# Order of the sliding attention's products, and 32-wide array strips for the RWKV head sums

## The reference, cut to what matters

```python
def swa_mixer(h, w_qkv, q_gain, k_gain, sinks, w_o, cos, sin):
    qkv = h @ w_qkv                      # 16 query heads, 4 key heads, 4 value heads of 64
    q = rope_slice(rms_norm(q, q_gain), cos, sin, 0)   # rope on the first 16 of 64 features
    k = rope_slice(rms_norm(k, k_gain), cos, sin, 0)
    # scores q k / 8, kept where |i - j| <= 128, softmax with a sink per head, times v
    return o @ w_o

# rwkv7_mixer
    kk = heads(k * k_k)
    kk = kk / jnp.maximum(jnp.sqrt(jnp.sum(kk * kk, axis=-1, keepdims=True)), 1e-12)
    # per direction:
    bonus = jnp.sum(rf * kd * rkf, axis=-1, keepdims=True) * vf    # 16 heads of 64
```

## Time and profile before

| | us |
|---|---|
| median of 3 runs | 1478.11 (1477.13 to 1478.13) |
| the profiled execution | 1479.16 |
| its span, first to last instruction | 1476.8 |
| PE busy in the span | 1418.9 |
| DVE, ACT, POOL busy | 549.3, 302.4, 115.1 |
| mean granted TensorE clock | 0.985 of 2.4 GHz |

### The profile page before, as it was taken

The page is one execution under the profiler, slowest core; times in us unless marked ns, Lnnn a source line. Parts: engine busy times, 40 slices in busy tenths (PEclk is TensorE's granted clock), DMA queues, the critical chain, the costliest instruction groups (busy, mean ns, idle before and its releaser), DMA issues.

```text
span 1476.8 us, 21440 instructions
## 1 busy us (share of the span) xinstructions
PE 1418.9 (96%) x9420; PEld 1027.3 (70%) x9420; DVE 549.3 (37%) x1032; ACT 302.4 (20%) x631; POOL 115.1 (8%) x180
## 2 busy tenths in 40 slices
PE   7999998999999997899999999999999989999999
PEld 6867567588884444468887458857788666888843
DVE  4677411121220045423333038448444372333300
ACT  3221102110110013411121003603433331212100
POOL 5654000000000000000000000022000000000000
PEclk9999999999999997999999999999999999999999
DMA  8343233244344334044434443400000222434432
GB/s 308 134 171 114 113 115 115 91 159 170 122 165 170 115 129 156 1 148 164 168 123 165 170 172 114 172 1 2 4 31 31 91 84 114 153 133 172 153 132 86
DMA packets 16605, 181.94 MB, mean 123 GB/s; under 512 B 1649, under 2 KB 3825, under 8 KB 5889
## 3 DMA queue, kind: packets, MB, share of 16 engines
q1 hardware_dynamic: 14320, 175.12, 31.4%
q10 hardware_dynamic: 2192, 5.46, 1.0%
HBM read 179.52 MB, written 1.05 MB: 122 GB/s over the span
## 4 chain that ended last, share of the span: by engine, by line
PE 89%; DVE 7%; ACT 3%; issue 1%; DMA 0%; POOL 0%; DVEq 0%; POOLq 0%
PE banks L1212 38%; PE banks L1475 15%; PE banks L1243 13%; PE banks L1222 4%; PE banks L1705 2%; PE banks L1426 2%; PE banks L1694 2%; PE banks L1198 1%; DVE weight_ring L2527 1%; PE banks L1563 1%; ACT weight_ring L1099 1%; ACT weight_ring L1104 1%; PE banks L1825 1%; PE banks L1776 1%; PE banks L1551 1%
## 5 line engine op out<-in xcount | busy, mean ns | idle before, releaser
L1212 PE MATMUL banks<-hT,weight_ring 128*128 128x256 f32 x2240 | 487.3, 379 | 1.0 <-DVE hT L1971 1.0
L1212 PEld LDWEIGHTS banks<-hT,weight_ring 128*128 128x128 f32 x2240 | 424.6, 190 | 62.2 <-issue 1.4
L1475 PE MATMUL banks<-weight_ring,arena 128*128 128x512 f32 x528 | 227.4, 592 | 0.0
L2256 DVE SCALAR_TENSOR_TENSOR arena<-banks,prm,arena 128x255 f32<-128x255 f32 x220 | 96.1, 478 | 305.4 <-ACT arena L944 197.2
L1475 PEld LDWEIGHTS banks<-weight_ring,arena 128*128 128x128 f32 x528 | 100.1, 190 | 124.1 <-issue 123.9
L1243 PE MATMUL banks<-weight_ring,arena 128*128 128x512 f32 x288 | 127.4, 600 | 3.0 <-ACT arena L1129 1.2
L1980 DVE TENSOR_TENSOR x<-x,banks 128x512 f32<-128x512 f32 x28 | 19.1, 686 | 276.5 <-PE banks L1475 192.2
L1243 PEld LDWEIGHTS banks<-weight_ring,arena 128*128 128x128 f32 x288 | 54.9, 192 | 69.7 <-issue 68.2
L944 ACT ACTIVATE arena<-banks,prm 128x256 f32<-128x256 f32 x66 | 33.6, 559 | 242.0 <-PE banks L1212 207.8
L1212 PE MATMUL banks<-arena,weight_ring 128*128 128x256 f32 x320 | 71.9, 386 | 0.0
L785 ACT ACTIVATE xn<-x 128x512 f32<-128x512 f32 x32 | 20.0, 627 | 242.5 <-DVE x L1980 236.6
(11 more groups left out here) (383 smaller groups left out, 1390.1 us busy)
## 6 DMA issues: line engine op xcount, KB each, us to landing
weight_ring<-in_wall SPq DMA_DIRECT2D x81, 2048.0 KB, 8.2
weight_ring<-in_wall SPq DMA_DIRECT2D x2, 1024.0 KB, 7.2
x<-in_x_tok ACTq DMA_DIRECT2D x2, 512.0 KB, 4.4
arena<-in_mem_tok SPq DMA_DIRECT2D x1, 1024.0 KB, 17.4
arena<-in_wall SPq DMA_DIRECT2D x1, 1024.0 KB, 5.0
arena<-in_wide SPq DMA_DIRECT2D x2, 512.0 KB, 4.9
out_y<-x ACTq DMA_DIRECT2D x4, 256.0 KB, 2.0
arena<-in_masks ACTq DMA_DIRECT2D x1, 896.0 KB, 9.9
```

The lines of the kernel that those rows point to most:

```text
L1212: ins = mm(b_(n)[:, j * T:(j + 1) * T], lhsT=wc[:, kb * 512 + c0:][:, :P], rhs=xT[:, kb, :], start=kb == 0, stop=kb == blocks - 1)
L1475: ins = mm(b_(tile_group(name, tt, c)), lhsT=actT[:, fb, tt * P:(tt + 1) * P], rhs=wc[:, (fb % 4) * D + c * 512:][:, :512], start=fb == 0, ...
L2256: ins = stt(out, src, col(f"fcw{i}", tap * nb_ + fb), out, ALU.mult, ALU.add)
```

## The change

Two parts.

Sliding attention. The qkv weights are laid out as keys and values (chunk 0), query heads 0 to 7 (chunk 1), query heads 8 to 15 (chunk 2). PE's order becomes: chunks 0 and 1 of tile 0, tile 1's norm transposes, chunks 0 and 1 of tile 1, chunk 2 of tile 0; then the transposes of the keys and of query blocks 0 and 1, for both tiles at once; then half of chunk 2 of tile 1 (`last_heads`), scores of units 0 and 1, the other half, and the loop. Query blocks 2 and 3 are transposed in the loop behind `window_columns(1)`. DVE's norm and rope become `head_norms(tt, h0, count)`: twelve heads (keys and eight queries) of each tile before the keys are copied out, eight heads of tile 0 before unit 0's maximum, eight heads of tile 1 between `window_p(0)` and `window_max(2)`. `w_sq` has a buffer for each tile, so that ACT no longer waits for `qk_sums`. ACT copies the last qkv group out between the exponentials of units 0 and 1. The groups have named banks.

RWKV. `headsel` gets 32 columns a block (the two heads of a block at 2 (fb mod 2), the rest zero), and `kk_ss` sums each of four pairs of blocks on its own strip of 32 array columns, into rows 32q of the bank. `kk_bc` takes its 32 rows from strip q and writes bank q. `bonus` works as `kk_ss` does, with 256 moving columns; DVE copies its 256 columns to `bonus_rows`, two transposes (`tx_bonus`, in level 2 of step 0) turn them to tokens, and DVE copies 32 columns of them to `r_bon` in level 3. POOL's clearing of the states waits for `tx_bonus` instead of `bonus`. The constants `cst` and `back` grow by 64 KB each.

```diff
@@ order of the groups
-    out += [("qkv_a", 2), ("tx_swa_b", 2), ("qkv_b", 4), ("k_tr", 1), ("q_tr", 4)]
-    out += [("sw_s0", 1, "pair0"), ("sw_s1", 1, "pair1")]
+    out += [("qkv_a", 2, 0, 1), ("tx_swa_b", 2, 2, 3), ("qkv_b", 3, 4, 5, 7), ("k_tr", 1, 6), ("q_tr_a", 2, 2, 3)]
+    out += [("sw_s0", 1, "pair0"), ("sw_s1", 1, "pair1"), ("qkv_c", 1, 6)]
     for u in range(8):
-        out += [(f"sw_s{u + 2}", 1, f"pair{u % 2}")] * (u < 6) + [(f"sw_t{u}", 1, "pair2")]
+        out += [(f"sw_s{u + 2}", 1, f"pair{u % 2}")] * (u < 6) + [(f"sw_t{u}", 1, "pair2")] + [("q_tr_b", 2, 7, 6)] * (u == 1)
@@ ScalarE
-            for u in range(2):
-                window_exp(u)
+            window_exp(0)
+            qkv_out(*QKV_ORDER[5])
+            window_exp(1)
@@ TensorE
+            def last_heads(blocks):
+
+                n, wc = tile_group("qkv", 1, 2), chunk("qkv", 2)
+                if blocks.start == 0:
+                    free(n)
+                for kb in blocks:
+                    ins = mm(b_(n), lhsT=h_mid[:, kb, P:T], rhs=wc[:, kb * 512:(kb + 1) * 512], start=kb == 0, stop=kb == KB - 1)
+                if blocks.stop == KB:
+                    ins.then_inc(psum_full, 1)
+
+            for q in range(2):
+                pe.wait_ge(*when_read(norm_group("swa", 0) + q))
+            for c in (0, 1):
+                heads_of_tile(0, c)
+            norm_transposes(5, 1, norm_group("swa", 1), xn)
+            for q in range(2):
+                pe.wait_ge(*when_read(norm_group("swa", 1) + q))
+            for c in (0, 1):
+                heads_of_tile(1, c)
+            heads_of_tile(0, 2)
+            pe.wait_ge(roped, 2)
+            turn_heads(G["k_tr"], 0)
+            for q in range(2):
+                turn_heads(turned_q(q), 256 + 256 * q)
...
+            last_heads(range(4))
+            pe.wait_ge(*when_read(G["k_tr"]))
             for u in range(2):
                 window_scores(u)
+            last_heads(range(4, KB))
             for u in range(8):
                 if u < 6:
                     window_scores(u + 2)
                 if u == 7:
                     swa_out(0, range(4))
                 window_columns(u)
+                if u == 1:
+                    pe.wait_ge(roped, 4)
+                    for q in (2, 3):
+                        turn_heads(turned_q(q), 256 + 256 * q)
...
-            for fb in range(KB):
-                ins = mm(b_(n)[0:16, 0:T], lhsT=c_("headsel", KB * 16)[:, 16 * fb:16 * fb + 16],
-                         rhs=kk_sq[:, fb * T:(fb + 1) * T], start=fb == 0, stop=fb == KB - 1)
+            for j in range(2):
+                for q in range(4):
+                    fb = 2 * q + j
+                    ins = mm(b_(n)[32 * q:32 * q + 32, 0:T], lhsT=c_("headsel", KB * 32)[:, 32 * fb:32 * fb + 32],
+                             rhs=kk_sq[:, fb * T:(fb + 1) * T], start=j == 0, stop=j == 1, tile_position=(0, 32 * q))
...
-                n = G["kk_bc"] + q
-                free(n)
-                for j in range(2):
-                    ins = mm(b_(n)[:, j * T:(j + 1) * T], lhsT=back[:, (2 * q + j) * P:][:, :P],
-                             rhs=rn_out, start=True, stop=True)
-                ins.then_inc(psum_full, 1)
+                free(G["kk_bc"] + q)
+            for j in range(2):
+                for q in range(4):
+                    rows_ = slice(32 * q, 32 * q + 32)
+                    ins = mm(b_(G["kk_bc"] + q)[:, j * T:(j + 1) * T], lhsT=back[rows_, j * P:(j + 1) * P],
+                             rhs=rn_out[rows_, :], start=True, stop=True, tile_position=(32 * q, 0))
+                    if j:
+                        ins.then_inc(psum_full, 1)
...
-            for tt in range(TT):
-                for fb in range(KB):
-                    ins = mm(b_(n)[:, tt * 16:(tt + 1) * 16], lhsT=rks[:, fb * T + tt * P:][:, :P],
-                             rhs=bonus_sel[:, 16 * fb:16 * fb + 16], start=fb == 0, stop=fb == KB - 1)
+            for j in range(2):
+                for q in range(4):
+                    fb = 2 * q + j
+                    ins = mm(b_(n)[32 * q:32 * q + 32, 0:T], lhsT=bonus_sel[:, 32 * fb:32 * fb + 32],
+                             rhs=rks[:, fb * T:(fb + 1) * T], start=j == 0, stop=j == 1, tile_position=(0, 32 * q))
...
+                    if (j, lv) == (0, 2):
+                        pe.wait_ge(*when_read(G["bonus"]))
+                        transposes(G["tx_bonus"], [bonus_rows[:, tt * P:(tt + 1) * P] for tt in range(TT)])
@@ VectorE
+            for tt in range(TT):
+                head_norms(tt, 0, 12)
             n = G["k_tr"]
             dve.wait_ge(psum_full, n + 1)
             ts_(w_kT, b3(n, 2, T), col("k_col"), None, ALU.mult).then_inc(bank_sem(n), 1)
...
+            head_norms(0, 12, 8)
...
             for u in range(8):
                 window_p(u)
+                if u == 0:
+                    head_norms(1, 12, 8)
                 if u < 6:
                     window_max(u + 2)
+                if u == 1:
+                    for q in (2, 3):
+                        n = turned_q(q)
+                        dve.wait_ge(psum_full, n + 1)
+                        ts_(w_qT[:, 2 * q:2 * q + 2, :], b3(n, 2, T), col("q_col"), None, ALU.mult).then_inc(bank_sem(n), 1)
...
-            V.tensor_copy(r_bon, b_(n, 32)).then_inc(bank_sem(n), 1)
+            V.tensor_copy(bonus_rows, b_(n, T)).then_inc(bank_sem(n), 1)
...
+                    if (j, lv) == (0, 3):
+                        n = G["tx_bonus"]
+                        dve.wait_ge(psum_full, n + 1)
+                        V.tensor_copy(r_bon.rearrange("p (t q c) -> p t q c", t=TT, q=4),
+                                      b3(n, TT, P).rearrange("p t (q c) -> p t q c", q=4)[:, :, :, 0:4]).then_inc(bank_sem(n), 1)
```

More of the change, by code:

```diff
@@ L2302, in _, with head_norms @@
             dve.wait_ge(in_swc, 16)
[L2303 to L2305 removed]
+            def head_norms(tt, h0, count):
+                for c in ((0, 1) if h0 == 0 else (2,)):
                     dve.wait_ge(*when_read(tile_group("qkv", tt, c)))
[L2307 to L2309 removed]
+                part, root = qss[:, 20 * tt + h0:][:, :count], qrs[:, 20 * tt + h0:][:, :count]
+                do(V.tensor_reduce(part, h64b(w_sq[:, tt, HD * h0:][:, :HD * count]), AX, ALU.add))
@@ L2310, in _ @@
                 do(ts_(part, part, 1 / HD, EPS, ALU.mult, ALU.add))
-                do(newton_root(qrs[:, 20 * tt:20 * tt + 20], part, qrt))
-                qk = h64b(qkv[:, tt, 0:1280])
-                do(tt_(qk, qk, spread(qrs[:, 20 * tt:20 * tt + 20], HD), ALU.mult))
-                rot = 2 * HALF_ROT
-                step(tt_(qk[:, 0:16, 0:rot], qk[:, 0:16, 0:rot], tiled(row("q_gain", rot), 16), ALU.mult))
-                do(tt_(qk[:, 16:20, 0:rot], qk[:, 16:20, 0:rot], tiled(row("k_gain", rot), 4), ALU.mult))
+                do(newton_root(root, part, qrt[:, 0:count]))
@@ L2317, in _ @@
+                qk = h64b(qkv[:, tt, HD * h0:][:, :HD * count])
+                do(tt_(qk, qk, spread(root, HD), ALU.mult))
+                rot, keys = 2 * HALF_ROT, 4 if h0 == 0 else 0
+                if keys:
+                    step(tt_(qk[:, 0:keys, 0:rot], qk[:, 0:keys, 0:rot], tiled(row("k_gain", rot), keys), ALU.mult))
+                do(tt_(qk[:, keys:count, 0:rot], qk[:, keys:count, 0:rot], tiled(row("q_gain", rot), count - keys), ALU.mult))
                 x1, x2 = qk[:, :, 0:HALF_ROT], qk[:, :, HALF_ROT:rot]
-                cos_ = tiled(swc[:, SWC["cos"] + tt * HALF_ROT:][:, :HALF_ROT], 20)
```

111 lines of the change are left out of this document (52 added, 59 removed).

## The result

The changed kernel takes 1459.3 us (median of 4 runs, 1458.0 to 1459.5) against 1478.1 for the kernel before: 18.8 us less, a ratio of 0.9872 with a 95% interval of 0.9855 to 0.9889. The forecast was 1465.4 with a range from 1460.5 to 1472.5, so the gain was larger than forecast, and outside the range. The profiled execution took 1459.16 us, with a span of 1457.3.

The account below looks back on a forecast made before the run. TensorE was taken as the bound (busy 96% of the span), with VectorE bounding the window loop. Attention -4.0 and RWKV strips -8.75 make -12.75 us, from 1479.16 for the profiled execution to a median of 1465.4; range 1460.5 to 1472.5.

Parts of the forecast that it names:

- Start: Sliding attention, before tile 1's norm transposes: two products instead of three no longer cover DVE's eviction, cost +1.0 us.
- first norms: Sliding attention: DVE's twelve-head norm takes 6.2 us, eight heads 5.3; PE waits 0.8 us, not 6.7.
- filling: Sliding attention: transposes, half products and first scores fill PE's time; scores 0 at 565.7 instead of about 577.4.
- The price: Window loop: two more eight-head norms of 5.3 us each on DVE; end at 605.9 instead of 611.4, gain 5.5.
- The clock in the attention: One half clock stays in the loop, one may move onto the tail: 1.5 us off the 5.5, leaving -4.0.
- The strips: RWKV before its core: `kk_ss`, `kk_bc` and `bonus` on four strips at 1.1 us each, -8.75 us in all.
- The wait for bank 7: Ahead of `bonus`: PE stands about 0.7 us while ACT copies out the fourth `rw_v` group.
- rival 3: `kk_ss` and `bonus`: column strips hide no weight loads, 2.3 us instead of 1.1 each, +2.4, 1467.8 us; chance 0.11.
- rival 4: RWKV strips do not run beside each other at all: RWKV +1.1, total -2.9, 1475.2 us; chance 0.04.
- rival 5: The 48 strip instructions: each product drains the array before the next strip, +6.7, 1484.8 us; chance 0.03.
- theory A of `strips_in_order`: Strip groups: products overlap only with neighbours in the order on other strips; 2.2 us a group, kernel 3.4 us longer.
- Rival 2: Window loop gives nothing, through DVE's queue, PE's moved gap and a clock fall: 0 instead of -4, 1469.4 us; chance 0.17.

Follow-up runs that it names:

- norm_before_loop: The changed kernel with the norm of tile 1's last eight heads put back ahead of the first window maximum, outside the loop: 1468.1 us.
- sums_first: The changed kernel with two of VectorE's four bonus steps moved behind the sums that TensorE waits for in the tail: 1457.4 us.
- strips_in_order: The changed kernel with both products of one strip issued one behind the other, in all three strip groups, instead of round the strips: 1460.3 us.
- before_tail_banks: The kernel before with RWKV banks named so that the last output projection gets banks 2 and 3 instead of 4 and 5: 1474.0 us.
- old_tail_banks: The changed kernel with RWKV banks named so that the last output projection gets banks 4 and 5 again: 1462.4 us.
- kk_bc_one_strip: The changed kernel with the broadcast's eight products all on array rows 0 to 31 instead of four strips: 1460.5 us.

## Why the prediction was wrong

- **Start, first norms, filling: right.** +0.99 against +1.0; the twelve-head norm 6.2 and the eight-head norm 5.2 on VectorE, as worked out; PE's wait 0.58 against 0.8; scores 0 at 564.85 against 565.7.
- **The price: right in kind.** VectorE's last division ends at 606.95, against 605.9: a gain of 4.4 where I had 5.5. `norm_before_loop` shows that the whole gain goes with the early start, 1.6 of it by way of the clock.
- **The clock in the attention: this term failed.** From 5.5 us I took 1.5 for a half clock that might move onto the tail, and wrote that the new order "keeps one such fall in the loop". Before had two late ones: 600.2 to 603.6, behind which VectorE waited 2.07 us for scores, and 610.4 to 613.8 on the values and the output projection. I saw only the second. The first was in the 4.0 us of old waits from which I took my 3.2, so the 1.5 charged it again. The changed kernel has one late half clock. The loop's end moved by 4.4 us and the stretch behind it shrank by 1.7 (22.27 to 20.61 from the seventh transposes to B). So the term was +1.5 and should have been -1.7, against which the loop's end fell 1.1 short. The sum is -6.1 where I had -4.0, beyond the bound of -5.5 that I set for the attention; only the range's lower end had counted this half clock (-1.7) on top. Where the one that stays falls makes no difference: in the `sums_first` profile it lies behind the loop (604 to 607.5), the loop ends 1.6 earlier, and A to B is the same 102.96. The ten profiles with the new order and no unused products all have one late half clock, and the five with both tiles' norms ahead of the loop have two. That the new order has one fewer is thus shown, why it has is not.
- **The strips: right.** `kk_ss` -2.55 for -2.5, `kk_bc` -2.57 for -2.5, its half clock -1.65 for -1.7, `bonus` -1.72 for -1.7, the products behind it -0.8 for -0.65; -9.26 in all for -8.75. The wait for bank 7 was foreseen at its size; that it came from the attention's part was not. "No row shows four strips of 32" was wrong, though. The S5 block of the kernel before has one: 16 products (32 instructions) of 32 result columns on four column strips, in 2.0 us, both products of a strip one behind the other. Eight products of the same shape in one place take 3.6:

```profile
L1635 PE MATMUL banks<-arena,weight_ring 128*32 128x256 f32 x16 | 3.6, 380 | 0.0
L1351 PE MATMUL banks<-arena 128*32 128x256 f32 x32 | 2.0, 384 | 0.0
```

That is 1.0 us for eight, and it spoke against rivals 3, 4 and 5, and against theory A of `strips_in_order`, before any run.

- **The tail: a missing term.** "Banks in the tail change too, but each waits for one that was read long before" was said of the attention's end. I did not follow the rotation to the last output projection, where the old banks were being read. -2.4 to -2.8 us by `before_tail_banks` and `old_tail_banks`, the half clock that goes with the wait included. The remaining 1.3 to 1.7 of the 4.1 go with a half clock that comes or not for the same instructions. That part could be a bound of the range at most, not a forecast.
- **Rivals.** Rival 2 (the loop gives nothing) is out by 6 us. Rival 3 (column strips hide no weight loads) is out: 1.07 us for `kk_ss` and `bonus`, and 0.87 for each group more. The rule behind it, in the Trainium skill's "TensorE: Matmul & The Clock Gate", Part 3 (The mechanism), does not hold for 32-column strips in this trace. Rivals 4 and 5 fell with the same rows.

By size, between the two spans: 19.5 - 12.75 = 6.75 us, of which 4.1 is the tail, 2.1 the attention (3.2 its clock, less the 1.1 at the loop's end), and 0.5 the strips. The medians differ by 0.7 less than the spans.

## What to carry to other kernels

When a change names banks or buffers anywhere in a rotation, list the new owner of every buffer to the end of the program and look for each place where the former owner is read late. Count every stretch of half clock around a changed loop, before and after, and price each by what waits behind it: one fall cost 1.6 us and another, twice as long, 0.9 in one kernel and 1.6 in the next. Filling waits of 1.8 to 6.6 us with unused products was worth 1.65 and 2.36 us here, after 0.9 us was lost because the last of them ran on too long. Before writing that no row shows a form, search the whole trace for its shape.

## What the runs showed of the hardware

- Eight products of 256 moving columns took 1.07 us on four column strips of 32 over the same rows, and 3.6 in one place (line 1635 of the kernel before); on four row strips of 32 they took 1.15, and 3.72 on one (`kk_bc_one_strip`). The order in which the strips are issued did not matter (1.09 to 1.17 us).
- The broadcast on 16 rows was followed by a granted clock of 0.5 for 3.4 to 6.8 us in five profiles, the same on 32 rows (with `tile_position`) was not in one (0.3 us apart in start). The old `kk_ss`, 3.63 us on all rows with 16 result columns, was followed by none in its four profiles.
- With the same instructions and a wait of 2.55 us, the clock fell in six profiles of the tail and not in four (16.3 or 14.64 us). With the wait at 0.29 us it stayed at 1.00 in all three profiles.
